# Reordered queues and buffers in a four-part decoder kernel: S5 reloads, an FFN's last pair, scores scaled by groups

## What is computed

```
# layer 0: latent attention, then ConvFFN; layer 1: S5 mixer, then ConvFFN
k, v = mla_keys_values(c_all, r_all)         # 4096 cached rows + 4 new, per sequence
   # k is RMS-normalised per head: its norm divides the scores
s = q @ k * QK_HEAD**-0.5 ; p = softmax(s) ; o = p @ v

u = h @ w_in                                  # S5, 64 groups of 16 channels
x = einsum('btgc,gpc->btgp', u, b_bar) ; scan over time with a complex decay
y = gelu(c @ s + d*u) ; g = y @ w_out ; out = g[:1024] * sigmoid(g[1024:])

u = h @ w_up ; c = conv3(u) + b               # ConvFFN, 2 x 2816 channels
y = (silu(c[gate]) * c[value]) @ w_down
```

## Time and profile before

| | before |
|---|---|
| median of 3 runs (lowest, highest) | 3253.87 us (3253.67, 3255.57) |
| time of the profiled execution, its span | 3256.93 us, 3254.8 us |
| PE busy, DVE, ACT, POOL | 91%, 58%, 29%, 14% of the span |
| granted TensorE clock, mean | 0.95 of full |

### The profile page before, as it was taken

The page is one execution under the profiler, slowest core; times in us unless marked ns, Lnnn a source line. Parts: engine busy times, 40 slices in busy tenths (PEclk is TensorE's granted clock), DMA queues, the critical chain, the costliest instruction groups (busy, mean ns, idle before and its releaser), DMA issues. The chain is left out here.

```text
span 3254.8 us, 54187 instructions
## 1 busy us (share of the span) xinstructions
PE 2974.4 (91%) x19178; PEld 2787.0 (86%) x19178; DVE 1896.0 (58%) x3536; ACT 959.3 (29%) x1661; POOL 450.8 (14%) x650
## 2 busy tenths in 40 slices
PE   7978989999997899999999977786989999999997
PEld 4646679888886799999999967776988999999997
DVE  2446657666664566666656656563227665666664
ACT  3434335544553322222212231112123221222221
POOL 1004111211120000000000036440000000000000
PEclk9989989999997899999999978887999999999999
DMA  3010022222220111111111132325111111111111
GB/s 105 28 20 2 33 76 77 69 65 66 70 68 27 40 51 49 43 44 52 39 45 39 33 118 65 63 50 167 40 45 59 40 39 45 45 45 45 52 33 65
DMA packets 262500, 175.40 MB, mean 54 GB/s; under 512 B 77961, under 2 KB 247642, under 8 KB 262058
## 3 DMA queue, kind: packets, MB, share of 16 engines
q1 hardware_dynamic: 262314, 173.03, 18.5%
HBM read 150.54 MB, written 22.29 MB: 53 GB/s over the span
## 5 line engine op out<-in xcount | busy, mean ns | idle before, releaser
L1581 PE MATMUL f_up<-f_h_hi,f_wu_hi 128*128 128x352 f32 x2112 | 459.9, 326 | 5.3 <-DVE f_wu_lo L2013 5.3
L1581 PE MATMUL f_up<-f_h_hi,f_wu_lo 128*128 128x352 f32 x2112 | 456.8, 324 | 0.0
L1581 PE MATMUL f_up<-f_h_lo,f_wu_hi 128*128 128x352 f32 x2112 | 456.4, 324 | 0.0
L1581 PEld LDWEIGHTS f_up<-f_h_hi,f_wu_hi 128*128 128x128 f32 x2112 | 361.7, 190 | 7.2 <-DVE f_wu_lo L2013 7.0
L1581 PEld LDWEIGHTS f_up<-f_h_hi,f_wu_lo 128*128 128x128 f32 x2112 | 364.2, 189 | 0.0
L1581 PEld LDWEIGHTS f_up<-f_h_lo,f_wu_hi 128*128 128x128 f32 x2112 | 360.2, 188 | 0.0
L1894 PE MATMUL f_down<-f_a_hi,f_wd_hi 128*128 (+1 forms) x1056 | 350.3, 332 | 7.7 <-DVE f_a_lo L2108 5.6
L1939 ACT ACTIVATE f_conv<-f_u_row,f_taps 128x1056 f32<-128x1056 f32 x88 | 111.8, 1271 | 785.2 <-DVE f_u_row L2047 785.2
L1894 PE MATMUL f_down<-f_a_hi,f_wd_lo 128*128 (+1 forms) x1056 | 342.0, 324 | 0.0
L1894 PE MATMUL f_down<-f_a_lo,f_wd_hi 128*128 (+1 forms) x1056 | 341.9, 324 | 0.0
L2115 DVE TENSOR_TENSOR resid<-resid,f_down 128x352 f32<-128x352 f32 x528 | 271.7, 519 | 112.2 <-PE f_down L1894 109.3
(11 more groups left out here) (369 smaller groups left out, 5616.9 us busy)
## 6 DMA issues: line engine op xcount, KB each, us to landing
f_wu<-ffn_w_up SPq DMA_DIRECT2D x88, 512.0 KB, 3.9
ca_ring<-cache_ckv SPq DMA_DIRECT2D x256, 128.0 KB, 2.0
f_wd<-ffn_w_down SPq DMA_DIRECT2D x44, 512.0 KB, 4.1
sg_w<-ssm_w_out SPq DMA_DIRECT2D x16, 512.0 KB, 3.8
s_spill<-resid SPq DMA_DIRECT2D x8, 528.0 KB, 7.0
s_u<-sm_ut SPq DMA_DIRECT2D x8, 528.0 KB, 5.3
sg_y_raw<-s_y SPq DMA_DIRECT2D x8, 528.0 KB, 5.7
resid<-s_spill SPq DMA_DIRECT2D x8, 528.0 KB, 8.1
```

The lines of the kernel that those rows point to most:

```text
L1581: mm = nc.tensor.matmul(out(c), w, x(c), start=(first and n == 0), stop=(last and n == 2))
```

## The change

Three stages are edited.

S5: SP's step becomes `send_u(i)`, `load_w(i+2)`, `send_y(i-2)`, `load_u(i)`. The output weights `cl` get a second buffer. ACT makes the next block's `w_hi` later in its step. Two small staging tiles move into the free `w`.

```diff
             for i in range(STEPS):
+                if there(i):
+                    send_u(i)
                 if there(i + 2):
                     load_w(i + 2)
-                if there(i):
-                    send_u(i)
-                if there(i - 1):
-                    load_u(i - 1)
                 if there(i - LAG_Y):
                     send_y(i - LAG_Y)
+                if there(i):
+                    load_u(i)
...
-                if m >= 1:
-                    pool.wait_ge(y_done, Y_PARTS * m)
+                if m >= 2:
+                    pool.wait_ge(y_done, Y_PARTS * (m - 1))
...
-                    tt(cl[:, i, :, :, :], both[:, 0, :, :, :], both[:, 1, :, :, :], (ADD, SUB)[i])
+                    tt(cl[m % 2][:, i, :, :, :], both[:, 0, :, :, :], both[:, 1, :, :, :], (ADD, SUB)[i])
...
-                if there(i + 2):
-                    high(i + 2)
                 if there(i - LAG_Y):
                     gelu(i - LAG_Y)
...
                         put_diag(i + 1)
+                if there(i + 2):
+                    high(i + 2)
                 if there(i - LAG_V):
                     keep_toeplitz(i - LAG_V)
```

```diff
+        wd_last = [x[:, :, :, :].rearrange("p j k q -> p j (k q)") for x in (wu_hi, wu_lo)]
...
                     if isinstance(g, int) and g == 0:
+                        turn_small()
                         spread_total()
                     up_tile(g * GJ, 1)
+                    if isinstance(g, int) and g == NPAIR - 1:
+                        up_tile(g * GJ + 1, 0)
+                        up_tile(g * GJ + 1, 1)
...
                     down_pair(g - 1)
-                if tiles_in(g):
+                if tiles_in(g) and not (isinstance(g, int) and g == NPAIR - 1):
                     up_tile(g * GJ + 1, 0)
                     up_tile(g * GJ + 1, 1)
...
-            turn_small()
             pairs(pe, step)
...
+                hi = down_weights(g)[0]
+                if hi is not wd_hi:
+                    act.wait_ge(up_done, 2 * (NT - 1) + jj + 1)
...
+                if isinstance(g, int) and g == NPAIR - 1:
+                    begin_conv(g * GJ + 1, 1)
+                    high_down(g, 0)
+                    gate(g, 1)
+                    high_down(g, 1)
+                    return
...
+            def last_tiles(g):
...
+                j += 1
+                all_parts(j, 0)
+                keep_u(j, 1)
+                near, near_new, far, far_new = parts(j, 1)
+                return {1: lambda: near(0), 3: lambda: near(1), 4: near_new, 6: lambda: far(0), 8: lambda: far(1), 9: far_new,
+                        11: lambda: multiply(j, 0), 13: lambda: multiply(j, 1), 16: lambda: low(j, 0), 18: lambda: low(j, 1)}
```

```diff
+                if p % GP == 1 and p > GP:
+                    group_square(b, p // GP - 1)
+                if p % GP == 3 and p > GP:
+                    scale_group(b, p // GP - 1)
...
+            def group_square(b, g):
...
+                dve.drain()
+                nc.vector.tensor_tensor(rms[:, 0, g % 2, :, :], ssum[:, b % 2, own, :],
+                                        ssum_pe[:, b % 2, own].unsqueeze(2).to_broadcast([P, GP, H]), ALU.add).then_inc(ms_done, 1)
+
+            def scale_group(b, g):
+
+                dve.wait_ge(sd_done, b * NG + g + 1)
+                nc.vector.reciprocal(rms[:, 2, g % 2, :, :], rms[:, 1, g % 2, :, :])
+                dve.drain()
...
+                nc.vector.tensor_tensor(flat, flat, rms[:, 2, g % 2, :, :].rearrange("p g h -> p (g h)").unsqueeze(2).to_broadcast([P, GP * H, NDEC]), ALU.mult)
+                dve.drain()
+                nc.vector.tensor_reduce(tops[:, g, :], cur.rearrange("p g c -> p c g"), AXX, ALU.max)
...
-                stream(b, page, {3: root, 6: keep_meanT, 14: exponentials})
+                stream(b, page, {2: last_root, 6: keep_meanT, 15: exponentials})
...
-                stream(b, page, {1: keep_part, 2: mean_square, 4: mean, 5: scale_scores, 6: column_top, 9: row_top, 12: shift})
+                stream(b, page, {1: begin, 3: last_group, 4: mean, 5: column_top, 9: row_top,
+                                 12: lambda b: shift(b, 0), 13: lambda b: shift(b, 1)})
```

More of the change, by code:

```diff
@@ L1404, in page @@
                     keep_kpeT(*next_group(b, p))
+                if p % GP == 2 and p > GP:
+                    root(b, p // GP - 1)
             def keep_kpeT(b, p):
@@ L1526, in scale_scores @@
-            def scale_scores(b):
-                if in_range(b, 1, NSEQ):
-                    s = (b - 1) % 2
-                    dve.wait_ge(sd_done, b)
-                    nc.vector.reciprocal(rms[:, 0, :, :], rms[:, 1, :, :])
-                    dve.drain()
-                    cur = scores[:, s, 0:NPAGE, :].rearrange("p g (h t) -> p (g h) t", h=H)
-                    nc.vector.tensor_tensor(cur, cur, rms[:, 0, :, :].rearrange("p g h -> p (g h)").unsqueeze(2).to_broadcast([P, NPAGE * H, NDEC]), ALU.mult)
+                if p % GP == 1 and p > GP:
+                    group_square(b, p // GP - 1)
@@ new lines, in begin, with last_group @@
+            def begin(b):
+                keep_part(b)
+                if in_range(b, 1, NSEQ):
+                    group_square(b - 1, NG - 1)
+                    new = s_new[:, b - 1, :, :].rearrange("p h t -> p (h t)")
+                    nc.vector.tensor_copy(scores[0:TS, (b - 1) % 2, NPAGE, :], new)
+                    nc.vector.tensor_copy(tops[0:TS, NG, :], new)
+            def last_group(b):
+                if in_range(b, 1, NSEQ):
+                    scale_group(b - 1, NG - 1)
@@ L1545, in row_top, with shift @@
                     nc.vector.tensor_scalar(top_diag[:, :], ident[0:QC, 0:QC], top_row[:, 0:1], None, ALU.mult).then_inc(diag_done, 1)
-            def shift(b):
+            def shift(b, part):
                 if in_range(b, 1, NSEQ):
                     dve.wait_ge(top_spread, b)
-                    cur = scores[:, (b - 1) % 2, :, :]
-                    nc.vector.tensor_tensor(cur, cur, misc[:, 0:QC].unsqueeze(1).to_broadcast([P, NPAGE + 1, QC]), ALU.subtract).then_inc(shifted, 1)
+                    own = slice(0, NPAGE // 2) if part == 0 else slice(NPAGE // 2, NPAGE + 1)
+                    cur = scores[:, (b - 1) % 2, own, :]
+                    nc.vector.tensor_tensor(cur, cur, misc[:, 0:QC].unsqueeze(1).to_broadcast([P, own.stop - own.start, QC]), ALU.subtract).then_inc(shifted, 1)
             def mean(b):
@@ L1719, in ffn, with down_weights, activations @@
         total = conv[:, 0, :]
+        wd_last = [x[:, :, :, :].rearrange("p j k q -> p j (k q)") for x in (wu_hi, wu_lo)]
+        def down_weights(g):
+            return wd_last if isinstance(g, int) and g == NPAIR - 1 else (wd_hi, wd_lo)
+        def activations(j):
+            return (h_hi[:, 0, :], h_lo[:, 0, :]) if isinstance(j, int) and j == NT - 1 else (a_hi[:, j % 3, :], a_lo[:, j % 3, :])
         h_hi_done = sem("h_hi_done")
@@ L1948, in gate @@
                 act.wait_ge(act_done, j + 1)
-                if not isinstance(j, int) or j >= 3:
+                if isinstance(j, int) and j == NT - 1:
+                    act.wait_ge(up_done, 2 * NT)
+                elif not isinstance(j, int) or j >= 3:
                     act.wait_ge(down_done, (g - 1 + jj) * NDP)
-                nc.scalar.activation(a_hi[:, j % 3, :], conv[:, 0, :], ACT.Copy).then_inc(a_hi_done, 1)
+                nc.scalar.activation(activations(j)[0], conv[:, 0, :], ACT.Copy).then_inc(a_hi_done, 1)
             act.wait_ge(gain_in, 16)
@@ L2107, in low @@
                     dve.wait_ge(a_hi_done, j + 1)
-                op = nc.vector.tensor_tensor(a_lo[:, j % 3, own], conv[:, 0, own], a_hi[:, j % 3, own], ALU.subtract)
+                hi, lo = activations(j)
+                op = nc.vector.tensor_tensor(lo[:, own], conv[:, 0, own], hi[:, own], ALU.subtract)
                 if side == 1:
@@ L2128, in step @@
                     between = {NCH * m + NCH - 1: lambda m=m: tail_sum(m - 1) for m in range(2, KT)}
-                if tiles_in(g):
+                ends = isinstance(g, int) and g == NPAIR - 1
+                if ends:
+                    between = last_tiles(g)
+                elif tiles_in(g):
                     j = g * GJ
@@ L2147, in step @@
                         part()
-                if tiles_in(g):
+                if tiles_in(g) and not ends:
                     j = g * GJ + 1
@@ L2595, in carried @@
                     rows = slice(a * NST, (a + 1) * NST)
-                    return nc.tensor.matmul(place(x, a), cl[rows, n, x, :, :], s[m % 2][rows, n, x, 0:OWN], start=False, stop=(n == 1))
+                    return nc.tensor.matmul(place(x, a), cl[m % 2][rows, n, x, :, :], s[m % 2][rows, n, x, 0:OWN], start=False, stop=(n == 1))
                 for x in range(GPB):
```

80 lines of the change are left out of this document (47 added, 33 removed).

## The result

The changed kernel takes 3157.8 us (median of 4 runs, 3149.4 to 3164.1) against 3254.1 us before; the ratio is 0.9698, 95% interval 0.9683 to 0.9713. That is 96 us less where 110 were predicted, and inside the range. The profiled execution took 3163.95 us for its span of 3162.0 us.

A forecast was written before the change was run, and what follows sets the result against it. PE, busy 91% of the span, and what it waits for bound the kernel. S5 55, FFN 27 and attention 28 sum to 110 us, so 3253.9 - 110 = 3144 us; 8 in 10 range 3125 to 3176.

The forecast's parts named there:

- The mechanism: S5: issuing load_u(i) in step i removes PE's 5.2 us wait and most of the low clock; step 25.4 us against 33.5.
- 5.2 x 0.44/0.70: S5 step: state_inputs at the higher clock falls from 5.2 us to about 3; 2.8 taken.
- The rival that DVE becomes the bound: S5: rotate meets POOL, a step takes 28 to 30 us; total about 3165 us; chance 0.2.
- 3 off for small waits behind DVE: S5 steps: 3 us subtracted from 40 us for five steps and 8 us for the first, leaving 45 us.
- The end: End of S5: earlier load_u(7) 4 us, shorter wait before last group_outputs 5, its clock 2.5; together 11.5 us.
- The waits of 8.3 and 2.8 us: Each FFN layer: PE's waits before turn_last and down_pair(10) go, 11.1 us a layer.
- the start: FFN start: the chain of squares and sums sheds three small copies from ACT's queue; 0.8 us, bounds 0 and 2.
- POOL beside DVE: FFN, down_pair(9): POOL's two subtractions for pair 10 may each hold DVE about 2 us; cost 1 us, bounds 0 and 4.
- DVE's additions late in `down_pair(9)`: FFN: listed among the signs that would show the forecast wrong; no size given.
- DVE's lumps: Cached attention: scale_scores and the 2.02 us maximum overfill DVE's free time; splitting into groups cuts 31.1 us of waits to 6.
- the sign of being right: Cached attention: PE's waits for scores under 8 us in sum would show the forecast right.
- the column maximum of the last sequence: Cached attention: PE's single 4.4 us wait; 3 us of it saved, as only one group is left before the maximum.

The follow-up runs named there:

- The experiment without them: The changed kernel with the cached attention copying the shifted scores instead of taking their exponential; 3131.8 us (2 runs), cached attention 557.6 us in place of 577.4.

## Why the prediction was right, and where its terms were off

**The total.** 110 us were booked, the medians gave 96 and the two profiled executions 93: 42.6 in S5, 23.6 in the FFN layers, 26.8 in the attention. The mechanisms of S5 and the FFN came as forecast; some terms were mis-sized, and in the attention the working was wrong.

**S5 (booked 55; 42.6 in the first profile, 55.0 in the median with these edits alone).** The mechanism held: the old queue order alone brings back 44 us, and steps of 25.2 us were measured where 25.4 were worked out. One term of that step was right by luck: 5.2 x 0.44/0.70 is 3.3 us and not the 2.8 that were taken, and 2.80 was measured. The rival that DVE becomes the bound did not come: PE is busy throughout the steady steps. Up to `group_outputs(0)` S5 gained 7 us where 8 were booked (71.4 us from its start, 78.4 before).

The mis-sized term is "3 off for small waits behind DVE": in the first profile it is 11 us, one wait of 3.65 us for `rotate(0)` and a half-speed stretch behind it. I had seen that POOL's first phases overlap `rotate(0)`, and left out that in this one step PE has no `group_outputs` to cover it. The first profile is the worst case, however. Six profiles have the S5 code of the changed kernel, and in them the step loses 11.0, 9.4, 1.7, 0.2, 0 and 0 us, 3.7 on average, and S5 takes 270.7, 260.9, 254.1, 252.2, 253.5 and 254.4 us. The wait is long (3.55 to 3.65 us) in the first three. In the other three the clock had fallen earlier, at `turn_gains(1)`, and the slower `project(2)` gave `rotate(0)` its time. So 3 us is near the average, but for another reason than the one given. The end was booked at 11.5 us: from `group_outputs(5)` to the gate's first load it gained 7.1 us in the first profile (69.3 to 62.2) and 13.7 to 15.1 in the other five. The difference is the clock in the last two `group_outputs`.

**FFN (booked 13.7 a layer; 12.3 and 11.3 in the first profile, 9.4 to 12.3 and 8.0 to 11.7 over nine).** The waits of 8.3 and 2.8 us went, and the start gave 1.0 us in layer 0 (43.0 instead of 44.0 to the second wait for weights) and none in layer 1. The mis-sized term is POOL beside DVE, booked at 1 us within 0 to 4: 2.8 us of waits, and in six of nine profiles a fall of the clock behind them that is worth about 2 us of layer 0. "DVE's additions late in `down_pair(9)`" was on the list of what would show the forecast wrong, and it came.

**Attention (booked 28; 26.8).** The sum is right by luck, since its working is not. I read all of the 31.1 us as DVE's lumps and left 6. But 13 of them stood behind ACT's exponential in the kernel before as well, and 16.7 are left where under 8 was the sign of being right. The scores' waits gave 14.4 us where 25 were booked, and the column maximum of the last sequence 4.0 where 3 were. What I had not counted made up for the rest: the clock in the stream (470 to 980 us) rose from 0.98 to 1.00, which is some 20 us at the lower level before and 3 after, so up to 8.5 us, and two waits for the squares went, 2.6 us. The Trainium skill (ScalarE: Activation LUTs, "What ACT_TABLE_LOAD costs") puts the load of a switch at 1.28 us, and the trace agrees (1.28). The drain of 1.38 us that it adds is not in the rows: the load of 678.50 ends at 679.78 and the root starts at 679.80. I had used the load only for the question whether there are more switches, and not for what the sixteen there are cost. The experiment without them gives 19.8 us.

**Left open:** why the same wait of 3.6 us is followed once by some 24 us at the lower level and once by 3, why the clock falls at `turn_gains(1)` in some executions only, and so most of the scatter between the executions of one kernel, which is 2 to 17 us here. That the new order of the FFN and the groups of the attention each make their gain is read from the waits that went; no experiment takes one of them out alone.
